# One weight stream for the second and the last layer: latents' norms between gate tiles, the last norm as a factor behind the projection, values token-major

## The reference, cut to what matters

```python
def mla_layer(...):                       # second layer
    z = rms_norm_2(x, norm_g) @ w_in      # 512 + 512 + 64 + 2048 columns
    cq, ckv, k_pe, gate = split(z)
    q = (rms_norm_2(cq, q_norm_g) @ w_q_up).reshape(b, s, 16, 192)
    kv = (rms_norm_2(ckv, kv_norm_g) @ w_kv_up).reshape(b, s, 16, 256)
    ...                                   # head norms, rotary part, attention
    return x + (o * silu(gate)) @ w_out

def diff_layer(...):                      # last layer
    z = rms_norm_2(x, norm_g) @ w_in
    q, k, v, gate = split(z)              # 2048 columns each; 8 heads
    q = rms_norm_2(q, q_gain); k = rms_norm_2(k, k_gain)
    o = diff_attend(q, k, v, pos, lam)    # softmax(q0 k0) - lam softmax(q1 k1)
    o = rms_norm_2(o, subln_g) * (1 - lam_init)
    return x + (o * silu(gate)) @ w_out
```

## Time and profile before

| | before |
|---|---|
| median of three runs | 3782.03 us (3780.08 to 3783.7) |
| the profiled execution | 3781.89 us |
| its span in the trace | 3779.3 us |
| outside the span | 2.6 us |
| PE busy | 91% of the span |
| mean granted clock of TensorE | 0.948 |

### The profile page before, as it was taken

How to read it: one execution, slowest core, us unless ns; L and a number is a source line. 1 busy time by engine, 2 the same in 40 slices (tenths; PEclk the granted TensorE clock), 3 DMA queues, 4 the chain that set the end, 5 groups by cost and what they waited for, 6 DMA issues and landing times. The chain is left out here.

```text
span 3779.3 us, 51202 instructions
## 1 busy us (share of the span) xinstructions
PE 3423.9 (91%) x21404; PEld 2648.3 (70%) x21404; DVE 1665.8 (44%) x2759; ACT 1196.0 (32%) x1831; POOL 104.8 (3%) x78
## 2 busy tenths in 40 slices
PE   4999999899999879459958999998799999999899
PEld 2877777677877758247835666686677777777577
DVE  3335555445554422352235655532543445444532
ACT  4113334332333211122323444422333333333321
POOL 1000000001101000010000000000100000000000
PEclk8999999999999889779978999999899999999999
DMA  5423333322111253234412111243322223322433
GB/s 172 129 69 87 92 89 93 89 61 76 59 47 54 86 150 111 91 96 110 119 50 72 45 42 52 95 120 109 87 84 75 88 84 89 90 74 87 135 106 100
DMA packets 513128, 336.54 MB, mean 89 GB/s; under 512 B 25162, under 2 KB 462893, under 8 KB 512278
## 3 DMA queue, kind: packets, MB, share of 16 engines
q1 hardware_dynamic: 507078, 322.91, 29.1%
q10 hardware_dynamic: 5840, 10.62, 0.8%
HBM read 282.21 MB, written 51.27 MB: 88 GB/s over the span
## 5 line engine op out<-in xcount | busy, mean ns | idle before, releaser
L670 PE MATMUL PS<-XH,WHT 128*128 128x512 f32 (+1 forms) x2528 | 1033.7, 409 | 89.0 <-DVE WLT L658 66.4
L672 PE MATMUL PS<-XH,WLT 128*128 128x512 f32 (+1 forms) x2528 | 999.6, 395 | 0.0
L671 PE MATMUL PS<-XL,WHT 128*128 128x512 f32 (+1 forms) x2528 | 993.7, 393 | 0.0
L658 DVE TENSOR_TENSOR WLT<-AR,WHT 128x1024 fp32r<-128x1024 f32 (+1 forms) x348 | 419.1, 1207 | 822.6 <-ACT WHT L652 822.4
L670 PEld LDWEIGHTS PS<-XH,WHT 128*128 128x128 f32 (+1 forms) x2528 | 479.4, 190 | 205.7 <-DVE WLT L658 68.5
L652 ACT ACTIVATE WHT<-AR 128x1024 fp32r<-128x1024 f32 (+1 forms) x348 | 360.7, 1039 | 665.2 <-PE PS L672 655.5
L671 PEld LDWEIGHTS PS<-XL,WHT 128*128 128x128 f32 (+1 forms) x2528 | 478.8, 189 | 110.9 <-issue 10.0
L672 PEld LDWEIGHTS PS<-XH,WLT 128*128 128x128 f32 (+1 forms) x2528 | 477.9, 189 | 110.3
L584 PE MATMUL PS<-XH,WHT 128*128 128x512 f32 (+1 forms) x656 | 258.7, 394 | 65.5 <-DVE WLT L541 65.5
L586 PE MATMUL PS<-XH,WLT 128*128 128x512 f32 (+1 forms) x656 | 259.0, 395 | 0.0
L585 PE MATMUL PS<-XL,WHT 128*128 128x512 f32 (+1 forms) x656 | 257.0, 392 | 0.0
(11 more groups left out here) (368 smaller groups left out, 4425.9 us busy)
## 6 DMA issues: line engine op xcount, KB each, us to landing
AR<-b_w_in SPq DMA_DIRECT2D x128, 512.0 KB, 4.0
AR<-w_in SPq DMA_DIRECT2D x122, 512.0 KB, 3.7
AR<-a_w_in SPq DMA_DIRECT2D x48, 512.0 KB, 5.1
AR<-w_out SPq DMA_DIRECT2D x32, 512.0 KB, 5.1
AR<-a_w_out SPq DMA_DIRECT2D x32, 512.0 KB, 4.0
AR<-b_w_out SPq DMA_DIRECT2D x32, 512.0 KB, 5.4
residual_scratch<-RES SPq DMA_DIRECT2D x3, 4096.0 KB, 15.5
proj_scratch<-STG ACTq DMA_DIRECT2D x40, 256.0 KB, 2.0
```

The costliest lines, as they stand in the source:

```text
L658: self.nc.vector.tensor_tensor(self.shaped(self.low, n), self.shaped(self.raw, n), f32(self.shaped(self.high, n)), ALU.subtract).then_inc( ...
L670: mm(out, wh, xh[:, k0 + c, :], start=(start and c == 0), stop=False)
L671: mm(out, wh, xl[:, k0 + c, :], start=False, stop=False)
L672: last = mm(out, wl, xh[:, k0 + c, :], start=False, stop=(stop and c == nk - 1))
```

## The change

The second layer's blocks 2 to 5 become one block, and block 6 goes. The weight units of `a_w_in`, of the latent layer and of the last layer stand in one stream, in the order of use.

- **Gate tiles.** `latent` begins with the 25 tiles of `a_w_in`. The 8 latent tiles stay in SBUF (`RAW`); their squares and sums stand behind the next tile, the two factors, the multiplications and the splits into `CH_` and `CL` (in the space of `RES`) behind tiles 5, 6, 9 and 10. The rotary key, then pair 0's keys and queries, stand behind tiles 9, 10, 13, 14 and 15. Only the gates go to DRAM, issued by SP.
- **Output tiles of the second layer.** DVE adds bank and residual; SP stores the sum to DRAM; ACT squares it and makes the high part of sum times `b_norm`; DVE makes the low part; POOL adds the 16 squares up in `ACC`.
- **Last layer.** It starts with `row_norm`: PE sums `ACC` over the features twice (the same number on all partitions, and one a token on each partition), ACT and DVE make the factors `RB` and `RC`. The projections run on the input without the factor, and DVE multiplies it in where it empties a bank.
- **Values.** Four units of 4 k-tiles and 256 columns a head; `tokens` puts them out token-major; `v_turned` and `v_copy` go. The gate's bank is emptied ahead of its sigmoid, and the product is a step of its own (`gate`).

The diff, cut to its core:

```diff
-    for i in range(NP):
+    for t in range(25):
+        for h in range(2):
+            if t == KPE_TILE:
+                rope = w[8 * P * h:8 * P * h + 8 * P, 2 * A_LORA:2 * A_LORA + 64]
+                AU[t, h] = st.pieces(8, [(rope, 64), (rope, 64)])
+            else:
+                AU[t, h] = st.add(w, t * P if t < KPE_TILE else (t - 1) * P + 64, 8 * h, 8)
+        if t == 13:
+            KU[0] = kv_unit(0, 0)
+        if t == 14:
+            QRU[0] = q_unit(0, AV, 64)
+            QNU[0] = q_unit(0, 0, AV)
...
+            def tile(t):
+                if t >= 2:
+                    pe.wait_ge(a_evac, t - 1)
+                for h in halves:
+                    st.matmuls(pe, AU[t, h], TBK[t % 2], k.XHT, k.XLT, 8 * h, h == 0, h == 1)
...
+            after = {t: [lambda t=t: mean_square(t - 1)] for t in range(1, 9)}
+            after.update({9: [rotary_key], 10: [rotary_key_swap], 13: [lambda: key(0, 0), lambda: key(0, 1), lambda: key_sums(0)],
+                          14: [lambda: key_factors(0, 0), lambda: key_factors(0, 1), lambda: rotary(0), lambda: query(0, 0)],
+                          15: [lambda: swap(0), lambda: rotary_sums(0), lambda: query(0, 1), lambda: query_sums(0)],
+                          AT - 1: [lambda: scores(0, 0)]})
+            for t in range(AT):
+                tile(t)
+                for f in after.get(t, ()):
...
+            def sigmoid(t):
+                g = t - KPE_TILE - 1
+                st.used(act, AU[t, 1])
+                if g >= 2:
+                    act.wait_ge(ev_out[g % 2], 16 * (g // 2))
+                A(GT[:, g % 2, :], TBK[t % 2][:, :], ACT.Sigmoid).then_inc(a_sig, 1)
...
+                act.wait_ge(o_evac, n + 1)
+                if n >= 2:
+                    act.wait_ge(o_acc, n - 1)
+                A(SQO[:, n % 2, :], RT[n % 6], ACT.Square).then_inc(o_sq, 1)
+                A(NHI[n], RT[n % 6], ACT.Copy, scale=k.prm("b_norm", n)).then_inc(o_hi, 1)
+
+        @block.gpsimd
+        def _(pool):
+            for n in range(KT):
+                pool.wait_ge(o_sq, n + 1)
+                if n == 0:
+                    nc.gpsimd.tensor_copy(ACC, SQO[:, 0, :]).then_inc(o_acc, 1)
+                else:
+                    pool.wait_ge(o_acc, n)
+                    nc.gpsimd.tensor_tensor(ACC, ACC, SQO[:, n % 2, :], ALU.add).then_inc(o_acc, 1)
...
+            def out_low(n):
+                dve.wait_ge(o_hi, n + 1)
+                STT(out=NLO[n], in0=RT[n % 6], scalar=k.prm("b_norm", n), in1=f32(NHI[n]), op0=ALU.mult, op1=ALU.subtract).then_inc(o_lo, 1)
...
+            def normed(x):
+                dve.wait_ge(a_sum, 4 * x + 4)
+                TS(RD[:, x, :], SB[x][:, :], 1.0 / A_LORA, EPS, ALU.mult, ALU.add).then_inc(a_mean, 1)
+                dve.wait_ge(a_root, x + 1)
+                V.reciprocal(RN[:, x, :], RN[:, x, :]).then_inc(a_rec, 1)
+                dve.wait_ge(a_rec, x + 1)
+                for c in range(4 * x, 4 * x + 4):
+                    STT(out=RAW[:, c, :], in0=RAW[:, c, :], scalar=k.prm(("q_norm", "kv_norm")[x], c % 4), in1=RN[:, x, :], op0=ALU.mult, op1=ALU.mult).then_inc(a_norm, 1)
...
+        for q in range(4):
+            st.add(w, (BV0 + 2 * h) * P, 4 * q, 4, 2 * P)
...
-            def v_turned(p, j):
-                pe.wait_ge(v_evac, evacs(p, 4 + j))
-                if j:
-                    pe.wait_ge(a_vt, 2 * p + 1)
-                else:
-                    pe.wait_ge(a_root, p + 1)
+            def value_unit(p, u):
+                for c in HALF:
+                    if u == 0:
+                        pe.wait_ge(v_evac, evacs(p, 2 + c))
+                    last = st.tokens(pe, U0 + 16 * p + 8 + u, FB[c], (2 * c, 2 * c + 1), XH, XL, 4 * u, u == 0, u == 3)
+                    if u == 3:
+                        last.then_inc(p_v, 1)
+                if u < 3:
+                    last.then_inc(st.s_used, 1)
+
+            def row_norm():
+                mm(OB[0][:, :], C("ones"), ACC, start=True, stop=True).then_inc(p_rs, 1)
                 for b in range(TB):
-                    last = nc.tensor.transpose(MB[:, blk(b)], VV[:, j, blk(b)], C("ident"))
-                last.then_inc(p_vt, 1)
+                    last = mm(OB[1][:, b:b + 1], ACC[:, blk(b)], C("ones", 0, 1), start=True, stop=True)
+                last.then_inc(p_rs, 1)
 
...
-                tile(p, 4)
-                tile(p, 5)
+                value_unit(p, 0)
+                value_unit(p, 1)
                 if a >= 0:
                     turned(a, 2)
+                value_unit(p, 2)
+                value_unit(p, 3)
                 sums(p, 1, 0, p_ksum)
                 if a >= 0:
                     scores(a, 3)
                 tile(p, 6)
                 key_factors(p)
-                v_turned(p, 0)
                 tile(p, 7)
                 if a >= 0:
                     turned(a, 3)
-                v_turned(p, 1)
...
-            def v_copy(p, j):
-                act.wait_ge(p_vt, 2 * p + j + 1)
-                if p >= 2:
-                    act.wait_ge(p_values, 2 * (p - 1))
-                Ac(VT[p % 2][:, j, :], MB[:, :], ACT.Copy).then_inc(a_vt, 1)
-
             def sigmoid(p, j):
-                act.wait_ge(st.s_used, 2 * (8 * p + 6 + j) + 2)
-                if p >= 2:
-                    act.wait_ge(v_oz, 2 * (p - 1))
-                Ac(Z[p % 2][:, j, :], FB[j][:, :], ACT.Sigmoid).then_inc(a_sig, 1)
+                act.wait_ge(v_evac, evacs(p, 6 + j))
+                if p:
+                    act.wait_ge(v_gate, 2 * p + j - 1)
...
-            for n in range(3):
-                st.split_high(act, n)
+            act.wait_ge(v_rs, 2)
+            Ac(RS, RB, ACT.Sqrt).then_inc(a_rs, 1)
+            Ac(RC, RC, ACT.Sqrt).then_inc(a_rs, 1)
...
+            def row_norm():
+                dve.wait_ge(p_rs, 2)
+                TS(RB, OB[0][:, :], 1.0 / D, EPS, ALU.mult, ALU.add).then_inc(v_rs, 1)
+                TS(RC, OB[1][:, 0:TB], 1.0 / D, EPS, ALU.mult, ALU.add).then_inc(v_rs, 1)
+                dve.wait_ge(a_rs, 2)
+                V.reciprocal(RB, RS).then_inc(v_rs, 1)
+                V.reciprocal(RC, RC).then_inc(v_rs, 1)
+                dve.wait_ge(v_rs, 4)
+
             def evac(p, i):
-                dve.wait_ge(st.s_used, 2 * (8 * p + i) + 2)
-                bank, c = FB[i % 2][:, :], i % 2
+                c = i % 2
+                if i in (4, 5):
+                    dve.wait_ge(p_v, 2 * p + c + 1)
+                    if p >= 2:
+                        dve.wait_ge(p_values, 2 * (p - 1))
+                    for j in HALF:
+                        b = 2 * c + j
+                        last = TS(VT[p % 2][:, b, :], FB[c][:, 2 * P * j:2 * P * j + 2 * P], RC[:, b:b + 1], None, ALU.mult)
+                    last.then_inc(v_evac, 1)
+                    return
+                st.used(dve, U0 + 2 * (8 * p + i) + 1)
                 if i < 4:
                     if p >= 2:
                         dve.wait_ge(p_scores, NS * (p - 1))
-                    V.tensor_copy((QN, KN)[i // 2][p % 2][:, c, :], bank).then_inc(v_evac, 1)
-                elif i < 6:
-                    if p:
-                        dve.wait_ge(p_vt, 2 * (p - 1) + c + 1)
-                    V.tensor_copy(VV[:, c, :], bank).then_inc(v_evac, 1)
+                    out = (QN, KN)[i // 2][p % 2][:, c, :]
                 else:
-                    dve.wait_ge(a_sig, 2 * p + c + 1)
-                    TTn(Z[p % 2][:, c, :], bank, Z[p % 2][:, c, :], ALU.mult).then_inc(v_evac, 1)
+                    out = Z[p % 2][:, c, :]
+                TTn(out, FB[c][:, :], RB, ALU.mult).then_inc(v_evac, 1)
+
+            def gate(p, c):
+                dve.wait_ge(a_sig, 2 * p + c + 1)
...
     w = dram["a_w_in_2"][0, :, :]
+    st = Stream(k, "m")
+    units = latent_units(st, w, dram["a_w_q_up_2"][0, :, :], dram["a_w_kv_up_2"][0, :, :], dram["a_w_out_2"][0, :, :])
+    last = diff_units(st, dram["b_w_in_2"][0, :, :], dram["b_w_out_2"][0, :, :])
+    res_out = k.sem("l2_res_out")
     with k.scope():
-        norm(k, KT, "a_norm", ahead=columns(w, 0), side=(k.sem("l2_res_out"), Angles(k)))
-        project(k, [(8, CQ0, columns(w, 0), P, None), (1, KPE0, columns(w, 1024, width=64), 64, None),
-                    (KT, AG0, columns(w, 1088), P, "silu")], KT, ahead=True)
-        norm(k, 4, "q_norm", src=CQ0)
-        norm(k, 4, "kv_norm", src=CKV0, dst=4)
+        norm(k, KT, "a_norm", prefetch=(st, res_out), side=Angles(k))
     with k.scope():
-        st = Stream(k, "m")
-        units = latent_units(st, dram["a_w_q_up_2"][0, :, :], dram["a_w_kv_up_2"][0, :, :], dram["a_w_out_2"][0, :, :])
-        latent(k, st, units)
-    if stop == "l2":
-        k.dump_res = True
-        return dump(k)
-    w = dram["b_w_in_2"][0, :, :]
-    st = Stream(k, "d")
-    for h in range(BH):
-        for c0 in (BQ0, BK0, BV0, BG0):
-            for c in range(2):
-                for half in (0, 8):
```

(13 more changed lines are left out.)

528 lines of the change are left out of this document (316 added, 212 removed).

## The result

| | before | after |
|---|---|---|
| median | 3782.86 us (4 runs, 3780.08 to 3785.38) | 3686.51 us (4 runs, 3682.05 to 3688.58) |
| the profiled execution | 3781.89 us | 3688.58 us |
| its span | 3779.3 us | 3686.8 us |

The ratio is 0.9744, with an interval of 0.9727 to 0.9761. The forecast was 3674 us with a range of 3663 to 3696, and 62% for 3667 to 3682.

A forecast was written before the change was run, and what follows sets the result against it. Matmuls on PE bound the stages, and nothing bounds their joints. Gains of 55.5 + 1.9 + 1.5 + 42.1 + 7.0 = 108.0 us off 3781.89 gave 3674 us, range 3663 to 3696.

The forecast's parts named there:

- joints A and B: Gate tiles' end to first scores, gain 55.5 us; second layer's last matmul to last layer's first, gain 42.1 us.
- three signs of being wrong: Any wait over 5 us in gate tiles, low clock behind each square, or value units over 22 us a head.
- rival 2: DVE's norm chain delays low parts, or row factor and distances hold the third tile: priced 12 us, 3686; 12%.
- Matmuls of joint A: PE work still needed between gate tiles' end and first scores: squares, swaps, keys, queries, one-column sums; 31.0 us.
- Waits of joint A: PE waits among gate tiles: key and query sums 1.45 and 1.44, rotary key 1.4, key half 0.9; 5.2 us.
- Clock of joint A: Low clock at rotary key, key sums and query sums among gate tiles, 1.6 us three times: 4.9 us.
- kinds of matmuls: Loss between matmuls of different kinds at 13 interludes among gate tiles, 0.17 us each: 2.2 us.
- rival 1: Clock falls at the squares between gate tiles too, 1.6 us at each of 13 interludes, 16 more: 3690; 12%.
- rival 5: Weight units loaded or split late through the gate phase, 122 us, no gain; 3% including other large losses.
- Rival 3: PE's waits and low-clock stretches among gate tiles (10 us of 43) mostly filled, kind changes free: 3664; 9%.
- Start of the stage: Behind the norm, 1024-column weight units let PE begin the first gate tile sooner after ACT: gain 1.9 us.
- Behind the pairs: First output tiles after the loop of pairs: weights rounded one unit further ahead remove a wait; gain 1.5 us.

The follow-up runs named there:

- experiment 7: Changed kernel with pair 0's keys and queries spread over gate tiles 13 to 18, rotary key's sums behind tile 10; 3666.67 us.
- experiment 2: Changed kernel with pair 0's query sums, root and factors one gate tile later (16 instead of 15); 3673.36 us.
- experiment 1: The changed kernel measured once more with no edit; 3688.24 us.
- experiment 4: Changed kernel where SP waits for the positions before issuing the first four weight loads; 3685.66 us.
- experiment 3: Changed kernel with the last layer's values feature-major again, with transposes and ACT copies as before; 3689.72 us.
- experiment 11: Changed kernel plus spread prologue, late row factor, positions before weight loads; 192-byte pad, arena 128 bytes shorter, one offset for all; 3645.48 us.
- experiment 12: The kernel before the change with only a 64-byte pad ahead of the arena; 3761.63 us, ratio 0.9943.
- 9: Changed kernel plus spread prologue, late row factor and positions before weight loads, with a 64-byte pad ahead of the arena; 3656.39 us.
- 10: The kernel of 9 with 64 more bytes behind the arena, so the weights lie 64 bytes further on; 3685.09 us.
- experiment 5: Changed kernel whose last layer reads the input's high part in place of the low part, leaving its share out; 3679.53 us.

## Why the prediction was right, and where it was not

The sign, the range and the two large terms held: joints A and B gave 91.3 us where 97.6 were forecast. Of 108.0 forecast, 92.4 came (spans 3779.3 and 3686.8), and 3686.5 lies outside the 3667 to 3682 to which the prediction gave 62%. Of its three signs of being wrong two came: a wait over 5 us in the gate tiles (7.4), and value units longer than 22 us a head (22.85). Heads were to be 0.9 us shorter and are 0.45 longer. That the time stayed in the range, and close to rival 2's 3686, is in part luck: 8 us came in the loop of pairs that nobody forecast, against 13.1 missing in the last layer.

- **Matmuls of joint A, 31.0.** Right: 29.7 in experiment 7, where PE waits for nothing, some 0.6 of it slow pace.
- **Waits of joint A, 5.2.** This step failed. The two of 1.2 and 0.9 us and the 1.45 at the key sums came as worked out, but at the query sums I carried over 1.44 us from a place where DVE had nothing else to do. Here six instructions stood ahead of the copy. With its clock, that wait cost 10 to 12 us (experiment 2), where my sum had about 3 for it. This is rival 2, chains longer than their cover, at another chain than those I named and with my price of 12.
- **Clock of joint A, 4.9, and kinds of matmuls, 2.2.** The 25 tiles and joint A took 325.12, so 48.4 beside the tiles: 29.7 matmuls, 11.0 waits (7.38, 1.45, 1.20, 0.94), 2 of slow pace, and some 6 at the low clock (in experiment 1 nothing and some 8). The clock cost time only behind waits: without them (experiment 7) 29.7 us are left against the 31.0 counted for the matmuls alone, so nothing for the 2.2 of changes of kind, for which no run shows a cost, or for sums of one column. That refutes rival 1, and rival 5 too: PE was never short of units there. Rival 3, less than counted, is out with the 48.4 for a forecast of 43.3. The stretch with the eight squares ran at a clock of 1.00:

```profile
1660.00:1770.00 110.00, 110.00 (x468) 87.57 (x467) 38.52 (x38) 29.59 (x34) 0.00 (x0) 1.00 0.35 93
```

- **Start of the stage, 1.9.** The edge itself was right (ACT 1651.45, PE 1653.89, so 2.44 us). What I missed stands in the norm: the four loads now issued beside it delay the positions, DVE's chain for the angles is on the norm's path, and 1.4 to 1.7 us go back (experiment 4).
- **Behind the pairs, 1.5.** The wait is gone. But this stretch gained 9.5, of which some 8 lie in the loop, whose code did not change. The matmuls are the same, and the clock is higher in every second pair or so. A pair before, and two after:

```profile
2187.89:2242.35 54.46, 53.10 (x252) 36.48 (x252) 32.50 (x59) 24.43 (x43) 0.00 (x0) 0.94 0.15 45
```

```profile
2083.22:2135.56 52.34, 51.17 (x253) 36.20 (x252) 32.39 (x59) 24.32 (x43) 0.00 (x0) 0.97 0.17 46
2135.56:2189.36 53.80, 52.62 (x253) 36.52 (x252) 32.39 (x59) 24.33 (x43) 0.00 (x0) 0.94 0.16 44
```

  In the shorter one the first scores, behind the query sums, take 2.95 us instead of 4.60 (`L2471` and `L2473`, from 2083.22 and from 2135.56). Which pairs are short differs from trace to trace. Why there are none among six of the kernel before stays open.
- **Joint B, 42.1.** 40.9 came. The chain of adds and join took 4.3 (forecast 3.9), `row_norm` 3.4 (2.7), and the third tile waited 1.2 (1.3 before), as forecast.
- **Values, 7.0.** 2.6 with the low parts in the same place (experiment 3). The turns cost 0.80 us a head instead of the 0.88 taken. The rest is the price of a 256-column matmul: I took 0.113 from three starts of one unit, and the layer has 0.119. The ends of -3 and +6 for it held: it came to +3.9. Rival 4, exposed weight loads, is out: 0.006 us a matmul are not 0.188. The Trainium skill ("TensorE: Matmul & The Clock Gate", Part 3) would, by the prediction's estimate from that page, have had 82 us here; the trace disagrees with it for these full-size loads.
- **The pace, not in the sum.** 8.6 us of the last layer, the largest single part of the miss, which my sum put at nothing. I took "same instructions, same duration" for granted, though the diff moves the low parts into the arena. Placed at one offset, the last layer goes at 227.4 ns (experiment 11).

So 108.0 - 92.4 = 15.6 is, within rounding: last layer 13.1 (pace 8.6, values 4.4), joint A 5.1, start 1.7, joint B 1.2, and 2.6 in untouched code ahead (there the `w_out` tiles' pace of 233.3 ns in this trace cost 3.4), less 8.0 more in the pairs.

## What to carry to other kernels

A wait between tiles cost more than its length here: 3.6 us of waits cost 6.3, and 7.4 cost 10 to 12, the rest being low clock. So put a full tile between a chain and the PE work that needs it. And find the length of the chain by reading the other engine's own order up to the instruction that ends it, not from a place where that engine was free. When operands move to other memory, count the matmuls in a window of a full stage before and after. If the clock is 1.00 in both and the number is not the same, look at where both operands begin.

## What the runs showed of the hardware that was not expected

- **The pace depends on where the operands lie.** By the sizes of the buffers in the kernel, the weights begin 147136 bytes of a partition behind the high parts, and the last layer's low parts, after the change, 96320 bytes behind them. With the difference taken within 256 bytes, moving rows less weights (64 and 128 there): 0 gives 226.7 ns, 64 gives 228.9, 192 gives 233.3, all in the same unedited loop. The last layer, with high parts at one offset and low parts at another, had 231.9 (64 and 128), 232.4 (0 and 128), 231.2 (192 and 64) and 227.4 (0 and 0); before the change it had 229.4 (64 and 64), and 227.3 with the pad (0 and 0). In time that is 21.7 us of 3783 for the kernel before (experiment 12), and 29 between two pads 64 bytes apart (9 and 10).
- **What is shown of it, and what is not.** Shown is that the place of the weights counts with the low parts left where they were (9 and 10), and the place of the low parts with the weights left where they were (9 and 11). That it is the difference, and not the two places by themselves, is not shown: the high parts began at the same byte in every run, so in the unedited loop a rule by the weights' place alone fits as well. Two more things stay open. At an offset of 64 the `w_out` tiles went at 233.3 in the trace of after and in that of experiment 4, and at 228.9 in eight others. And experiment 5, which reads only at 64 in the last layer, had 230.0 there and not 229.4. Nor is one offset the best for all: the 256-column value units took 23.19 us a head in experiment 11 and 22.85 after the change.
- The Trainium skill ("TensorE: Matmul & The Clock Gate", Part 2, Step-by-step: what each phase is for) says that loading the next weights takes no SBUF bandwidth from the running matmul, since PE has two read ports. Loads do run beside matmuls here (0.188 us each, beside value matmuls that start 0.119 apart). But where the operands lie changes the time by up to 3% (226.7 to 233.3), which that sentence does not lead one to expect; whether the loads' reads are what slows the matmuls, no run shows.
- **A right number is no proof.** Experiment 9 met its forecast within the microsecond by a mechanism that its own trace refutes.
